# First stream's scores in banks of their own, its value low halves behind the next stream's third key chunk, masks among the prompt's last outputs

## The reference

```python
def layer(x, prev_k, prev_v, prev_logf, ...):
    h = rmsnorm(x, norm_g)
    pu, pg, q, k, v, ag, fl, cb, cc, cx, cgate = split(h @ w_in)
    a = pooled means of pu, mixed by pool_w and gated by silu(pg)
    q, k = rmsnorm(q), rmsnorm(k)
    F = cumsum(concat(prev_logf, log_sigmoid(fl + b_f)))
    o = attend(q, concat(prev_k, k), concat(prev_v, v), F)
    b = o * silu(ag)
    c = short convolution of cc * cx, times cb, gated by silu(cgate)
    return x + concat(a, b, c) @ w_out, k, v, logf, new states

def attend(...):
    s = q . k * scale + F_query - F_key      # masked to key position <= query position
    return softmax(s) @ V
```

## Time and profile before

| | |
|---|---|
| median of 3 runs | 1571.77 us (1565.47 to 1574.16) |
| profiled execution, its own time | 1569.85 us |
| its span | 1568.1 us |
| granted TensorE clock, mean | 0.992 |
| busy: TensorE, VectorE, ScalarE, GpSimd | 97%, 57%, 42%, 29% |
| streams' attention, roughly | 1203 to 1376 us of the span |

### The profile page before, as it was taken

The page is one execution under the profiler, slowest core; times in us unless marked ns, Lnnn a source line. Parts: engine busy times, 40 slices in busy tenths (PEclk is TensorE's granted clock), DMA queues, the critical chain, the costliest instruction groups (busy, mean ns, idle before and its releaser), DMA issues.

```text
span 1568.1 us, 24740 instructions
## 1 busy us (share of the span) xinstructions
PE 1514.4 (97%) x9212; PEld 1339.2 (85%) x9212; DVE 892.2 (57%) x2145; ACT 654.6 (42%) x1379; POOL 455.7 (29%) x736
## 2 busy tenths in 40 slices
PE   8999999999999999999999999999998899998999
PEld 8997878878899899998888888888887787777887
DVE  4333112242444423224888988988987788787663
ACT  5443121121211201114977877877876444432220
POOL 2110005555400000113444444444433345322221
PEclk9999999999999999999999999999999999999999
DMA  4533123122100201312233233232323656633442
GB/s 160 154 108 97 49 83 105 47 74 75 56 33 20 71 19 38 75 30 50 50 70 70 52 68 67 54 68 63 54 86 124 206 197 219 236 119 138 161 155 88
DMA packets 177288, 144.65 MB, mean 92 GB/s; under 512 B 103887, under 2 KB 136560, under 8 KB 177168
## 3 DMA queue, kind: packets, MB, share of 16 engines
q1 hardware_dynamic: 174656, 134.08, 29.2%
q10 hardware_dynamic: 2448, 8.91, 1.4%
q0 software_dynamic: 64, 0.07, 0.1%
HBM read 106.50 MB, written 36.53 MB: 91 GB/s over the span
## 4 chain that ended last, share of the span: by engine, by line
PE 70%; DVE 9%; POOL 7%; issue 6%; ACT 4%; DMA 4%; SPq 0%; POOLq 0%; DVEq 0%; ACTq 0%
PE banks L949 18%; PE banks L943 13%; PE banks L2612 8%; PE banks L1581 6%; PE banks L1572 4%; PE banks L1567 3%; POOL in_h_rstd L521 3%; PE banks L1597 3%; PE banks L1598 3%; POOL in_out L526 2%; PE banks L2058 2%; PE banks L1550 2%; PE banks L2039 2%; ACT pa_s_ring L1421 2%; DVE in_out L779 1%
## 5 line engine op out<-in xcount | busy, mean ns | idle before, releaser
L943 PE MATMUL banks<-in_w_hi,in_xt_hi 128*128 128x512 f32 (+1 forms) x680 | 240.7, 354 | 3.6 <-DVE in_w_lo L677 1.8
L943 PE MATMUL banks<-in_w_hi,in_xt_lo 128*128 128x512 f32 (+1 forms) x680 | 238.1, 350 | 0.0
L943 PE MATMUL banks<-in_w_lo,in_xt_hi 128*128 128x512 f32 (+1 forms) x680 | 237.3, 349 | 0.0
L1471 DVE CUSTOM_DVE_ANT_0 pa_s_ring<-banks,pa_f_b 128x512 f32<-128x512 f32 (+2 forms) x320 | 193.1, 603 | 35.6 <-PE banks L1572 32.3
L1519 DVE TENSOR_TENSOR pa_pt_lo<-banks,pa_pt_hi 128x512 fp32r<-128x512 f32 (+2 forms) x320 | 193.0, 606 | 21.0 <-ACT pa_pt_hi L1450 18.4
L949 PE MATMUL banks<-in_xt_hi,in_w_hi 128*128 128x384 f32 (+1 forms) x576 | 194.2, 337 | 5.6 <-DVE in_w_lo L677 5.4
L949 PE MATMUL banks<-in_xt_hi,in_w_lo 128*128 128x384 f32 (+1 forms) x576 | 190.0, 330 | 0.0
L949 PE MATMUL banks<-in_xt_lo,in_w_hi 128*128 128x384 f32 (+1 forms) x576 | 189.6, 329 | 0.0
L1450 ACT ACTIVATE pa_pt_hi<-banks 128x512 fp32r<-128x512 f32 (+2 forms) x320 | 166.6, 534 | 54.1 <-PE banks L1581 53.1
L1581 PE MATMUL banks<-ident,pa_s_ring 128*128 128x128 f32 x1088 | 174.0, 275 | 9.6 <-DVE pa_pt_lo L1519 4.3
L1597 PE MATMUL banks<-pa_pt_hi,pa_vs 128*128 128x256 f32 x576 | 163.6, 300 | 0.4 <-DVE pa_parts L1499 0.3
(11 more groups left out here) (298 smaller groups left out, 2918.4 us busy)
## 6 DMA issues: line engine op xcount, KB each, us to landing
sa_k_c<-in_cache_k_dram SPq DMA_DIRECT2D x8, 2048.0 KB, 9.1
sa_v_c<-in_cache_v_dram SPq DMA_DIRECT2D x8, 2048.0 KB, 8.2
in_w_raw<-in_w_in_dram SPq DMA_DIRECT2D x40, 256.0 KB, 4.0
out_dram<-in_out SPq DMA_DIRECT2D x34, 256.0 KB, 2.0
out_dram<-op_x ACTq DMA_DIRECT2D x17, 512.0 KB, 3.1
op_x<-in_x_prompt_dram SPq DMA_DIRECT2D x16, 512.0 KB, 3.9
in_x<-in_x_prompt_dram SPq DMA_DIRECT2D x14, 512.0 KB, 3.6
pa_f_b<-scratch_f SPq DMA_DIRECT2D x28, 256.0 KB, 5.2
```

What stands on the lines that cost most here:

```text
L943: mm = pe.matmul(ps[:, u % NBANK, 0:n], tile_of(xa, t)[:, k, :], wa[:, k, c0:c0 + n], start=(k == 0 and q == 0), stop=(k == KT - 1 and q = ...
L1471: done = dve.tensor_tensor_reduce(scores_of(j)[:, b * P:(b + nb) * P], ps_s[:, (h * NQD + at) % 3, 0:nb * P], f_b[h % 2][:, b * P:(b + nb) ...
```

## The change

Three edits, all where the streams' attention begins:

- VectorE's constants move into a step "consts" of the streams' `on_dve`, which the prompt's `on_dve` calls ahead of its last `invert_sums`. The step waits for 10 of GpSimd's `made` counts instead of 14 (the last four are memsets of other tensors).
- The scores of stream 0 go to banks 6, 7 and 3 (`ps_f`), those of the other streams stay in 2, 4 and 5. Scores of stream 1 wait for no exponentials any more; those of stream 2 and later wait as before. Banks 3 and 7 held the prompt's outputs, so the wait `outputs_gated` goes from `turn_p(0, ...)` to ahead of stream 0's first score, and ScalarE gets the wait `stores_landed` behind `high_k(1, 2)`.
- `low_v(0, ...)` moves out of stream 0's round, into stream 1's, behind `low_k(1, 2)` and the first minimum, ahead of `low_p(0, (0, 1))`. The later streams' stay where they are.

```diff
--- before.py
+++ after.py
@@ -1459,7 +1459,7 @@
         for g in (NG - 2, NG - 1):
             copy_output(H - 1, g)
 
-    def on_dve(dve):
+    def on_dve(dve, following):
         def take_chunk(h, j, n):
 
             if n == 0 and j == 0:
@@ -1526,6 +1526,7 @@
                         ended = pair_ended(h, j - 1, LAG)
                         if ended:
                             gate_output(*ended)
+        following("consts")
         invert_sums(H - 1, NJ - 1)
         for g in (NG - 2, NG - 1):
             gate_output(H - 1, g)
@@ -1710,6 +1711,7 @@
     v_n = m.at(210048, "v_n", [P, DA])
     ps_k = m.banks(0, 2)
     ps_s = [m.banks(n, n + 1)[:, 0, :] for n in (2, 4, 5)]
+    ps_f = [m.banks(n, n + 1)[:, 0, :] for n in (6, 7, 3)]
     ps_o = m.banks(3, 4)[:, 0, :]
     ps_p = m.banks(6, 8)
 
@@ -1747,6 +1749,10 @@
 
         return (b - par) * (unit // 2) + unit
 
+    def scores(b, c):
+
+        return (ps_s if b else ps_f)[c][:, 0:WID[c]]
+
     def on_sp(sp, step, weights):
         def by_head(rows, b):
 
@@ -1906,7 +1912,7 @@
         def exps(b, par):
             act.wait_ge(row_min, b + 1)
             for c in range(NC_):
-                act.activation(p[par][:, OFF[c]:OFF[c] + WID[c]], ps_s[c][:, 0:WID[c]], ACT.Exp,
+                act.activation(p[par][:, OFF[c]:OFF[c] + WID[c]], scores(b, c), ACT.Exp,
                                scale=-1.0, bias=low[:, par, 3:4],
                                accum_out=rsum[:, par, c:c + 1]).then_inc(exp_done, 1)
 
@@ -1915,6 +1921,8 @@
 
         for b in range(NB):
             high_k(b, 2)
+            if b == 1:
+                prompt.stores_landed(act)
             if b:
                 high_p(b - 1, (0, 1))
             if b + 1 < NB:
@@ -1927,18 +1935,20 @@
         weights()
         high_p(NB - 1, (0, 1, 2))
 
-    def on_dve(dve, weights):
-
-        dve.wait_ge(made, 14)
-        dve.tensor_tensor(later[:, :, :], later[:, :, :],
-                          own[:, :].rearrange("p (h o) -> p h o", o=1).to_broadcast([P, H, NQ]),
-                          ALU.mult).then_inc(rounded, 1)
-        dve.wait_ge(rounded, 1)
-        dve.tensor_reduce(mask_f[:, :], later[:, :, :].rearrange("p h q -> p q h"), AX_X,
-                          ALU.add).then_inc(rounded, 1)
-        dve.wait_ge(rounded, 2)
-        dve.tensor_copy(mask_b[:, :], mask_f[:, :]).then_inc(rounded, 1)
-        dve.tensor_copy(sel[:, :], sel_f[:, :]).then_inc(rounded, 1)
+    def on_dve(dve, step, weights):
+        if step == "consts":
+            dve.wait_ge(made, 10)
+            dve.tensor_tensor(later[:, :, :], later[:, :, :],
+                              own[:, :].rearrange("p (h o) -> p h o", o=1).to_broadcast([P, H, NQ]),
+                              ALU.mult).then_inc(rounded, 1)
+            dve.wait_ge(rounded, 1)
+            dve.tensor_reduce(mask_f[:, :], later[:, :, :].rearrange("p h q -> p q h"), AX_X,
+                              ALU.add).then_inc(rounded, 1)
+            dve.wait_ge(rounded, 2)
+            dve.tensor_copy(mask_b[:, :], mask_f[:, :]).then_inc(rounded, 1)
+            dve.tensor_copy(sel[:, :], sel_f[:, :]).then_inc(rounded, 1)
+            return
+
         dve.wait_ge(q_turned, 1)
         dve.tensor_copy(q_t[:, :, :].rearrange("p a r -> p (a r)"), ps_s[0][:, :]).then_inc(q_copied, 1)
 
@@ -1967,7 +1977,7 @@
 
         def minima(b, par, c):
             dve.wait_ge(scored, b * NC_ + c + 1)
-            dve.tensor_reduce(low[:, par, c:c + 1], ps_s[c][:, 0:WID[c]], AX_X, ALU.min).then_inc(chunk_min, 1)
+            dve.tensor_reduce(low[:, par, c:c + 1], scores(b, c), AX_X, ALU.min).then_inc(chunk_min, 1)
 
         def output(b, par):
 
@@ -1998,6 +2008,9 @@
             par = b % 2
             low_k(b, 2)
             minima(b, par, 0)
+            if b == 1:
+                for quarter in range(4):
+                    low_v(0, 0, quarter)
             if b:
                 low_p(b - 1, (0, 1))
             if b + 1 < NB:
@@ -2010,8 +2023,9 @@
             minima(b, par, 2)
             dve.wait_ge(chunk_min, b * NC_ + NC_)
             dve.tensor_reduce(low[:, par, 3:4], low[:, par, 0:3], AX_X, ALU.min).then_inc(row_min, 1)
-            for quarter in range(4):
-                low_v(b, par, quarter)
+            if b:
+                for quarter in range(4):
+                    low_v(b, par, quarter)
             if b == NB - 1:
                 low_p(b, (0, 1))
             if b:
@@ -2042,15 +2056,18 @@
 
         def score(b, par, c, ahead):
 
-            out = ps_s[c][:, 0:WID[c]]
+            out = scores(b, c)
             if c == 0:
                 pe.wait_ge(f_in[par], count(b, par, 32))
                 pe.wait_ge(qz_done, 2 * b + 2)
 
-            wait_some(pe, exp_done, NC_ * b - (NC_ - 1 - c))
+            if b == 0 and c == 0:
+                prompt.outputs_gated(pe)
+            if b >= 2:
+                pe.wait_ge(exp_done, NC_ * b - (NC_ - 1 - c))
             pe.matmul(out, sel[:, :], f_s[:, par, OFF[c]:OFF[c] + WID[c]], start=True, stop=False)
             if c == NC_ - 1:
-                pe.matmul(ps_s[c][:, 2 * P:2 * P + NQ], ident_b[:, :], mask_b[:, :], start=False, stop=False)
+                pe.matmul(out[:, 2 * P:2 * P + NQ], ident_b[:, :], mask_b[:, :], start=False, stop=False)
             for n in range(NP):
                 pe.wait_ge(kt_l, b * KB + c * NP + n + 1)
                 z = slice(n * P, (n + 1) * P)
@@ -2062,8 +2079,6 @@
                 ahead(n)
 
         def turn_p(b, par, part):
-            if b == 0:
-                prompt.outputs_gated(pe)
             if part[0] == 0:
                 pe.wait_ge(exp_done, b * NC_ + NC_)
             for n in part:
@@ -2713,8 +2728,8 @@
         @block.vector
         def _(dve):
             first.dve(dve)
-            prompt.dve(dve)
-            sample.dve(dve, lambda finish: last.dve(dve, finish))
+            prompt.dve(dve, lambda step: sample.dve(dve, step, None))
+            sample.dve(dve, None, lambda finish: last.dve(dve, finish))
 
         @block.tensor
         def _(pe):
```

## The result

The changed kernel takes 1574.62 us (median of 20 runs, 1572.63 to 1578.29) against 1568.81 us before (20 runs, 1565.47 to 1575.36): a ratio of 1.0035, with a 95% interval of 1.0025 to 1.0045. That is 5.5 us more, between 3.9 and 7.1. The profiled execution took 1574.54 us with a span of 1572.8, where before it was 1569.85 and 1568.1: + 4.7.

The account below looks back on a forecast made before the run. TensorE, busy 97%, bounds most stages; here the value loop has no slack. Low halves ending 5.0 us later swallow both gains: net + 5.0 on the 1571.77 median gives 1576.8 us, range 1570 to 1583.

Parts of the forecast that it names:

- Part 1: Masks moved into VectorE's idle time before the prompt's last inversion: TensorE's restart and stream 0 come 0.7 us earlier.
- Part 2: Stream 0's scores in other banks: the 2.50 us stall before stream 1's scores goes; third key turn at 1226.0, before 1229.18.
- nothing of VectorE stands in front of it any more: Stream 1's third key turn, at 1226.0, waits for ScalarE's copy and its remainder, with no other VectorE work ahead.
- Part 3: Stream 0's value low halves moved into stream 1: they end 5.0 us later, delaying stream 1's value load; net + 5.0.
- The landing: Stream 1's value load, from issue to GpSimd's start: 9.77 us, with bounds of - 0.7 to + 0.2.
- The minimum of stream 1: On VectorE, before stream 1's low halves: 1.2 us later, at 1242.1, after which VectorE waits 5 us for GpSimd.
- the second replaces the one already there: TensorE's stall of about 6 us before stream 2's third key chunk replaces the existing 2.5 us one; sum stays + 5.
- a longer idle time costs no more than a short one: TensorE's clock after its stalls: once it is down, longer idling adds nothing, so the sum stays at + 5.
- So all of it stays: Later streams to the end: nothing makes up the 5 us, since the value load and VectorE move together.
- A: Stream 1's values come in time anyway and TensorE reaches stream 0's probabilities earlier: - 3.4 us, or 1568.4; chance 0.12.
- B: Stream 2's first chunks run longer at 1.2 GHz after the 6 us stall: + 8 to + 9, or 1580; chance 0.18.
- C: TensorE stops as long at stream 1's third key chunk behind ScalarE's exponentials: + 6; chance within the forecast's 0.70.

Follow-up runs that it names:

- e3: Kernel before with only VectorE's masks moved ahead of the prompt's last inversion; banks, waits and low halves as before; ratio 1.0010.
- e1: Changed kernel with stream 0's value low halves back in their old place, so only masks and banks changed; 1568.61 us against 1570.78, ratio 0.9987.
- e2: Kernel before with only stream 0's scores in banks 6, 7 and 3, with their waits; masks and low halves as before; ratio 1.0005.
- e4: Kernel before with only stream 0's value low halves moved, plus ScalarE's added wait for the prompt's stores; 1581.26 us against 1570.78, ratio 1.0079.
- e5: Kernel before, with SP's load of stream 1's values also waiting for stream 0's second probability remainder; 1578.32 us against 1570.57, ratio 1.0041.
- e12: The changed kernel itself, measured again later; 1574.56 us, ratio 1.0026 to the kernel before.
- e9: Changed kernel, stream 0's low halves made as zeros, stream 1's values loaded early, GpSimd's high halves held until VectorE's low halves end; 1569.53 us against 1571.06.
- e7: Kernel before, with stream 0's low halves made as zeros from the high halves and stream 1's values loaded without waiting for them; 1568.04 us, ratio 0.9983.
- e8: Kernel before with masks and banks changed, two of stream 0's four low-half instructions on GpSimd, two on VectorE in the old place; 1567.11 us against 1570.57.
- e6: Changed kernel, with stream 0's low halves made as zeros from the high halves and stream 1's values loaded without waiting for them; 1574.32 us, ratio 1.0022.
- e11: e8 with 4 and 10 dummy matmuls of 384 columns in TensorE's two stalls; 1568.24 us, ratio 0.9978 to the kernel before.

## Why the prediction was right

The forecast was + 5.0 us; the runs gave + 5.5 (3.9 to 7.1) and + 4.1 (1.9 to 6.4), the trace + 4.7. The mechanism is the one forecast. The time itself, 1576.8, was 2.2 too high: it stood on a median of three runs, 1571.77, where twenty runs of the kernel before give 1568.81. By its own steps, with 0.49 taken off:

| step | forecast | measured |
|---|---|---|
| first remainder of stream 0 | 1204.8 | 1204.83 |
| third turn of stream 1's third chunk | 1226.0 | 1226.06 |
| low halves of stream 0 | 1229.0 to 1233.6 | 1229.06 to 1233.68 |
| load of stream 1's values | 1233.7 | 1233.76 |
| GpSimd's high halves | 1243.5 | 1243.74 |
| VectorE reaches low_v(1) | 1242.1 | 1243.56 |
| low_v(1) starts | 1247.1 | 1247.41 |
| VectorE's idle time before it | 5 | 3.85 |
| key remainder of stream 2 (the chain's row) | 1255.9 | 1256.13 |
| TensorE's stall near 1231 | about 4 | 4.19 |
| TensorE's stall before 1256 | about 6 | 5.09 |

**Part 1** gave what was forecast in the trace: minimum 0 came 0.65 us earlier. As a part alone it did not show in the runs (e3).

**Part 2** was right for the whole change: no stall before stream 1's scores, and the third turn held up by ScalarE's exponentials, whose key copies start at 1225.55 (1225.06 less the 0.49, forecast 1225.1). By itself the edit only moves the stall behind the low halves (3.69 us in e1 and e2); my later expectation of 1 to 1.5 for e2 had overlooked that VectorE is at the low halves then, though the prediction's own sentence for the whole change, "nothing of VectorE stands in front of it any more", implies it.

**Part 3** was right in place and size. The load leaves 5.07 us later behind the gating, low_v(1) starts 5.28 later, and TensorE restarts 5.26 later. The landing took 0.2 more than the row I used (9.98 from issue to GpSimd's start against 9.77), inside the bounds. The low halves took 4.62 and not up to 6.17, since GpSimd was quiet, as argued.

**Terms that were mis-sized.** The minimum of stream 1 was forecast 1.2 us later and came 2.66 later (1243.56 against 1240.90): the clock behind the 4.19 us stall was 0.57 for 4 us, which I had counted as hidden. It was hidden, so only waits shrank, VectorE's from 5 to 3.85 and TensorE's before 1256 from 6 to 5.09. And "the second replaces the one already there" was too kind: the slow stretch behind 5.09 us of idle time is 7.0 us long, not the 5.6 behind 2.47, which is 0.7 us of work more at half speed. That agrees with the rest of the trace: minimum 2 is 5.81 later than before, 0.55 more than the restart. The Trainium skill ("TensorE: Matmul & The Clock Gate", What's actually happening) says that activity releases the throttle; that a longer idle time costs no more than a short one was my reading, not its words. The traces don't tie the length of a slow stretch to the idle time ahead of it. The kernel before and e4 have the same stall of 2.5 us at the same place, 1224.93 and 1225.12, and e5 has one of 7.83 us that ended at 1262.14. Two windows of the kernel before:

```profile
1228.00:1230.00 2.00, 2.00 (x8) 1.47 (x9) 1.31 (x3) 0.41 (x2) 0.00 (x0) 0.59 0.08 16
1230.00:1232.00 2.00, 2.00 (x15) 1.77 (x16) 0.92 (x3) 1.10 (x3) 0.00 (x0) 1.00 0.82 253
```

Two of e4:

```profile
1232.00:1236.00 4.00, 4.00 (x17) 3.87 (x18) 3.38 (x5) 1.59 (x3) 0.00 (x0) 0.50 0.00 0
1236.00:1240.00 4.00, 1.88 (x11) 1.52 (x11) 4.00 (x6) 0.98 (x2) 0.00 (x0) 0.93 0.13 24
```

Two of e5:

```profile
1264.00:1268.00 4.00, 4.00 (x17) 3.44 (x17) 2.09 (x4) 1.59 (x3) 0.00 (x0) 0.50 1.05 352
1268.00:1272.00 4.00, 4.00 (x32) 3.70 (x30) 2.17 (x5) 2.11 (x5) 2.63 (x1) 0.97 1.03 376
```

Both slow stretches behind 2.5 us began near 1226; before it was over by 1230, in e4 only behind 1236. Behind 7.83 us it lasted 6 us, less than behind 5.09. So the 1.4 us more in the changed kernel are what its trace shows (e12's too), and no price of a longer stall.

**"So all of it stays"** was nearly right. Of the 5.8 us at minimum 2, 4.9 are left at low_v(7) and 4.2 at the end of the span; in e12's trace 5.8, 5.7 and 4.4. So about 1.5 us are given back in both, at different places: where, and by what, is not shown. That the sum fits so well is in part luck, since two misses cancel: at minimum 2 the lateness is 0.8 us above the forecast's 5.0, and at the end 0.6 to 0.8 below it.

**Rivals.** A (the gain stays) fell with the load, which leaves at the end of the moved instructions, and a free buffer would not have made it true either. e9's - 2.0 looks like A's - 3.4, but the kernel before with the same early load (e7) has - 2.7: the gain is the early load's, and the moved instructions add nothing to it. B (the clock grows the loss to 8 or 9) did not happen: it needed a slow stretch twice as long, and it was 1.25 times. The nearest to it is e4, where the third chunk runs at the lower clock for over 8 us and the loss is 12.4; its larger part is the place of the low halves (8.4 of the 9.26 us by the expectation), and the rest fits the clock. C was only half right: the bank stall moved to the third turn, but with 1.38 us and not its full length.

## What to carry to other kernels

Before moving an instruction to fill a stall, look at what it releases: here the last reader of a single buffer let SP start a 9 us load, and 5 us of delay there outweighed every stall that the move took away. Here an edit that brought this reader forward, by giving half of it to an idle engine (e8), gained 3.5 us where reordering the work around it lost 4 to 5.5. And when a wait is cut in an experiment, check what now runs at the same time, and compare with a control that has the same cut but not the change (e7 for e9): an early load started GpSimd beside VectorE and hid the answer (e6) until the two were kept apart (e9).

## What the runs showed of the hardware

**VectorE and GpSimd in the on-chip memory together.** The same four subtractions with two SBUF inputs took 4.62 us with GpSimd quiet (e9, e7, the changed kernel's stream 0), 6.17 beside its small instructions (the changed kernel's stream 1), and 9.43 beside its 3.62 us scaling and two small ones (e6). GpSimd's rows beside the 6.17:

```profile
1247.95 1.65 POOL L1877 TENSOR_SCALAR sa_v_hi<-sa_v_n 16x512 fp32r<-16x512 f32 x1
1249.68 2.12 POOL L1880 TENSOR_TENSOR sa_v_lo<-sa_v_n,sa_v_hi 16x512 fp32r<-16x512 f32 x1
1251.87 1.11 POOL L1865 CAST sa_qz_hi<-sa_q_t 64x64 fp32r<-64x64 f32 x1
1253.07 1.18 POOL L1867 TENSOR_TENSOR sa_qz_lo<-sa_q_t,sa_qz_hi 64x64 fp32r<-64x64 f32 x1
```

GpSimd is slowed as well: in e9, with VectorE not at such subtractions, the same four take 0.61, 1.27, 0.23 and 0.32 us. In e6 the scaling, which had started 0.13 us earlier, kept its length (3.62), and the two small ones took 1.46 and 2.10. If VectorE stood still for the 3.49 us that were left of the scaling and then took 6.17, it would be 9.66: an estimate, close to the 9.43. The Trainium skill ("SBUF — State Buffer", Who interferes with whom) says that a VectorE instruction with two SBUF inputs contends with a GpSimd instruction that reads SBUF; these rows agree, and put the price for VectorE at 1.3 to 2 times the length.

**GpSimd at a plain subtraction** of 128x1024 takes 2.36 us (4.71 for two, e8) where VectorE takes 1.16 (4.62 for four).

**TensorE's clock at the start of this stage differs between executions.** e5 gives TensorE the same instructions up to there as the kernel before, with the same waits, and its stalls there are the same to 0.01 us for the first two (1.49 and 0.70). Before, the granted clock was 1.00 from 1210 to 1222, in e5 0.57, and minimum 0 came 3.64 us later. In e3 it was 0.50 from 1210 to 1223, in e11 0.60 from 1212 to 1228, where the changed kernel had 1.00 and minimum 0 some 5 us earlier. This is as large as the effects studied here, and it may be one source of the spread of the runs (1565.47 to 1575.36 before). So two traces of this stage can be compared only row by row, and what a kernel gains or loses is told by many runs.
